# Block 2's expert loop: ScalarE and VectorE each split two neighbouring weight chunks in one operation of 2048 columns instead of one chunk in an operation of 1024

## The reference, cut to what matters

```python
def run_block(args):
    tok, e = args
    xb = hf[jnp.minimum(tok, n_tok - 1)]
    a = xb @ w_gate[e]
    b = xb @ w_up[e]
    return (jax.nn.silu(a) * b) @ w_down[e]
```

## Time and profile before

| | us |
|---|---|
| time before, median of 3 runs | 2129.56 |
| lowest and highest run | 2127.35 and 2130.23 |
| span of the profiled execution, first to last instruction | 2122.2 |
| TensorE matmul busy in it | 2024.8 (95%) |
| VectorE busy | 1678.8 (79%) |
| ScalarE busy | 1229.4 (58%) |
| GpSimd busy | 468.0 (22%) |

### The profile page before, as it was taken

How to read it: one execution, slowest core, us unless ns; L and a number is a source line. 1 busy time by engine, 2 the same in 40 slices (tenths; PEclk the granted TensorE clock), 3 DMA queues, 4 the chain that set the end, 5 groups by cost and what they waited for, 6 DMA issues and landing times.

```text
span 2122.2 us, 31552 instructions
## 1 busy us (share of the span) xinstructions
PE 2024.8 (95%) x9690; PEld 1676.1 (79%) x9690; DVE 1678.8 (79%) x1905; ACT 1229.4 (58%) x1453; POOL 468.0 (22%) x368
## 2 busy tenths in 40 slices
PE   5999999969999999999999999999999999999996
PEld 4888888858888878787778787888888888887873
DVE  6676755488999999999856455548999999999994
ACT  5211113216888787878644533224888888888872
POOL 1000001101010101010010253111344444444442
PEclk9999999959999999999999999999999999999998
DMA  9476844439999999999821112355999999999996
GB/s 353 143 233 220 266 179 167 174 135 338 380 379 388 377 389 377 390 377 390 319 75 54 37 41 105 114 186 203 384 383 383 370 381 378 372 378 363 379 361 242
DMA packets 234184, 592.52 MB, mean 279 GB/s; under 512 B 23936, under 2 KB 61076, under 8 KB 234109
## 3 DMA queue, kind: packets, MB, share of 16 engines
q1 hardware_dynamic: 210400, 527.50, 66.4%
q0 software_dynamic: 22640, 61.32, 9.8%
q10 hardware_dynamic: 1068, 2.73, 0.3%
HBM read 560.57 MB, written 50.91 MB: 288 GB/s over the span
## 4 chain that ended last, share of the span: by engine, by line
PE 64%; DMA 15%; DVE 8%; SPq 6%; issue 3%; ACT 2%; POOL 0%; POOLq 0%; ACTq 0%; DVEq 0%
PE ps L2377 19%; PE ps L2380 18%; PE ps L2378 18%; DMA ring<-in_moe_w_up 6%; SPq L575 6%; DMA ring<-in_w_expert_up 4%; DMA ring<-in_moe_w_down 1%; DVE mL L2301 1%; PE ps L2862 1%; PE ps L2532 1%; DVE mL L1777 1%; PE ps L2693 1%; DMA ring<-in_ada_w 1%; PE ps L2385 1%; DVE mL L2217 1%
## 5 line engine op out<-in xcount | busy, mean ns | idle before, releaser
L2217 DVE TENSOR_TENSOR mL<-ring,mH 128x1024 fp32r<-128x1024 f32 x384 | 479.3, 1288 | 21.6 <-ACT mH L1381 20.0
L1777 DVE TENSOR_TENSOR mL<-ring,mH 128x1024 fp32r<-128x1024 f32 x384 | 455.3, 1220 | 32.3 <-ACT mH L1189 22.8
L1189 ACT ACTIVATE mH<-ring 128x1024 fp32r<-128x1024 f32 x384 | 401.9, 1062 | 100.0 <-PE ps L2380 65.0
L1381 ACT ACTIVATE mH<-ring 128x1024 fp32r<-128x1024 f32 x384 | 394.9, 1056 | 65.4 <-PE ps L2380 21.5
L2377 PE MATMUL ps<-mH,xsH 128*128 128x512 f32 x1056 | 423.0, 401 | 2.2 <-DVE mL L2217 1.4
L2380 PE MATMUL ps<-mH,xsL 128*128 128x512 f32 x1056 | 413.3, 391 | 0.0
L2378 PE MATMUL ps<-mL,xsH 128*128 128x512 f32 x1056 | 411.0, 389 | 0.0
L2380 PEld LDWEIGHTS ps<-mH,xsL 128*128 128x128 f32 x1056 | 198.2, 188 | 43.5
L2377 PEld LDWEIGHTS ps<-mH,xsH 128*128 128x128 f32 x1056 | 198.7, 188 | 41.3 <-DVE mL L2217 1.6
L2378 PEld LDWEIGHTS ps<-mL,xsH 128*128 128x128 f32 x1056 | 198.9, 188 | 38.1
L2377 PE MATMUL ps<-mH,hidH 128*128 128x512 f32 x528 | 209.7, 397 | 7.8 <-DVE hidL L1832 6.4
(11 more groups left out here) (474 smaller groups left out, 3209.0 us busy)
## 6 DMA issues: line engine op xcount, KB each, us to landing
ring<-in_w_expert_gate SPq DMA_DIRECT2D x140, 512.0 KB, 11.2
ring<-in_w_expert_up SPq DMA_DIRECT2D x140, 512.0 KB, 11.4
ring<-in_w_expert_down SPq DMA_DIRECT2D x140, 512.0 KB, 12.5
ring<-in_moe_w_gate SPq DMA_DIRECT2D x128, 512.0 KB, 12.2
ring<-in_moe_w_up SPq DMA_DIRECT2D x128, 512.0 KB, 12.1
ring<-in_moe_w_down SPq DMA_DIRECT2D x128, 512.0 KB, 13.3
ring<-in_ada_w SPq DMA_DIRECT2D x96, 512.0 KB, 7.2
ring<-in_sc_w_in SPq DMA_DIRECT2D x24, 512.0 KB, 9.0
```

Source lines behind the costliest of these rows:

```text
L1189: act.activation(mH[:, m % WSETS, :], ring[:, m % RING, :], ACT.Copy).then_inc(S["m1_hi"], 1)
L1381: act.activation(mH[:, wset, :], ring[:, slot, :], ACT.Copy).then_inc(S["m2_hi"], 1)
L1777: dve.tensor_tensor(mL[:, m % WSETS, :], ring[:, m % RING, :], mH[:, m % WSETS, :].bitcast(F32), ALU.subtract).then_inc(S["m1_lo"], 1)
L2217: dve.tensor_tensor(mL[:, wset, :], ring[:, slot, :], mH[:, wset, :].bitcast(F32), ALU.subtract).then_inc(S["m2_lo"], 1)
```

## The change

`m2_hi` and `m2_lo` now take two neighbouring chunks, n and n + 1 with n even, in one operation of 2048 columns. The high part waits for both landings and for the buffers of both (n + 1 - 6 multiplied); `m2_hi` and `m2_lo` count by two when the whole operation is done. Both are called for even c alone. `EARLY2` goes from 3 to 2; in the opening ScalarE makes 0 and 1, then 2 and 3, then after the token's high parts 4 and 5, and VectorE makes 0 and 1 before the last routing operations and leaves 2 and 3 to the loop's step 0. What stands before an odd c stays where it was in the order, so silu and the hidden product now follow the pair (0, 1), and the first token part follows the pair (8, 9). The overflow blocks, TensorE, GpSimd and SyncE are left as they are.

```diff
--- before.py
+++ after.py
@@ -19,7 +19,7 @@
 RING = 12
 SPLIT_RING = 6
 EARLY1 = 4
-EARLY2 = 3
+EARLY2 = 2
 ADA_RING = 6
 WSETS = 6
 E1 = 16
@@ -1375,12 +1375,13 @@
 
         def m2_hi(q, r, c):
             n, slot, wset, turn = m2_at(q, r, c)
-            act.wait_ge(ring_in[slot], 16 * (used2[slot] + turn + 1))
+            for u in range(2):
+                act.wait_ge(ring_in[slot + u], 16 * (used2[slot + u] + turn + 1))
             if not (static(q) and n < WSETS):
-                act.wait_ge(S["m2_used"], n - WSETS + 1 + past["m2_used"])
-            act.activation(mH[:, wset, :], ring[:, slot, :], ACT.Copy).then_inc(S["m2_hi"], 1)
-
-        for c in range(EARLY2):
+                act.wait_ge(S["m2_used"], n + 1 - WSETS + 1 + past["m2_used"])
+            act.activation(mH[:, wset:wset + 2, :], ring[:, slot:slot + 2, :], ACT.Copy).then_inc(S["m2_hi"], 2)
+
+        for c in range(0, EARLY2, 2):
             m2_hi(0, 0, c)
 
         def x_hi2(e, r, j):
@@ -1398,11 +1399,10 @@
                            scale=slot_w[:, bass.ds(e, 1)]).then_inc(S["m2_y"], 1)
 
         act.wait_ge(S["tok_tr"], 2 + past["tok_tr"])
-        for c in (3, 4):
-            m2_hi(0, 0, c)
+        m2_hi(0, 0, 2)
         for j in range(2):
             x_hi2(0, 0, j)
-        m2_hi(0, 0, 5)
+        m2_hi(0, 0, 4)
         act.wait_ge(S["rows_known"], 1)
 
         def m2_step(q, r):
@@ -1424,7 +1424,7 @@
                                    ACT.Copy).then_inc(S["m2_hT_hi"], 1)
                 if c in (9, 11) and not (static(q) and s >= E2):
                     x_hi2(s + 1, 1 - r, (c - 9) // 2)
-                if not (static(q) and (s == 0 and c < WSETS or s == E2 and c < 8)):
+                if c % 2 == 0 and not (static(q) and (s == 0 and c < WSETS or s == E2 and c < 8)):
                     m2_hi(q, r, c)
             if static(q) and s == 0:
                 for j in range(2):
@@ -2213,9 +2213,9 @@
 
         def m2_lo(q, r, c):
             n, slot, wset, _ = m2_at(q, r, c)
-            dve.wait_ge(S["m2_hi"], n + 1 + past["m2_hi"])
-            dve.tensor_tensor(mL[:, wset, :], ring[:, slot, :], mH[:, wset, :].bitcast(F32),
-                              ALU.subtract).then_inc(S["m2_lo"], 1)
+            dve.wait_ge(S["m2_hi"], n + 2 + past["m2_hi"])
+            dve.tensor_tensor(mL[:, wset:wset + 2, :], ring[:, slot:slot + 2, :], mH[:, wset:wset + 2, :].bitcast(F32),
+                              ALU.subtract).then_inc(S["m2_lo"], 2)
 
         def x_lo2(e, r, j):
             dve.wait_ge(S["m2_xT_hi"], 2 * e + j + 1 + past["m2_xT_hi"])
@@ -2245,8 +2245,6 @@
                                       op0=ALU.mult, op1=ALU.add))
         dve.tensor_copy(row_of[:, 0:NBLK], slot_t[:, 1, :]).then_inc(S["rows_known"], 1)
         dve.wait_ge(S["rows_known"], 2)
-        for c in range(1, EARLY2):
-            m2_lo(0, 0, c)
         for j in range(2):
             x_lo2(0, 0, j)
 
@@ -2274,7 +2272,7 @@
                     x_lo2(s + 1, 1 - r, (c - 9) // 2)
                 if c == 11 and static(q) and s == E2 - 1:
                     hidden(s, r)
-                if not (static(q) and (s == 0 and c < EARLY2 or s == E2 and c < 8)):
+                if c % 2 == 0 and not (static(q) and (s == 0 and c < EARLY2 or s == E2 and c < 8)):
                     m2_lo(q, r, c)
             if static(q) and s == 0:
                 for j in range(2):
```

## The result

The changed kernel takes 2136.32 us (median of 5 runs, 2133.44 to 2137.61) beside 2129.24 us for the kernel before in runs shared with it: a ratio of 1.0038, with a 95% interval of 1.0027 to 1.0050. It is slower, by 0.38% or some 8 us (7.1 between the two medians). The time lies in the forecast's range, but the loss isn't the 1 us of the forecast, and it is more than the 0.2% that I had called no change. The profiled execution has a span of 2131.8 us, 9.6 more than before. A run's time is 1.6 us longer than its span (2133.44 us for this one), so the profiled execution of the kernel before would be a run of 2123.8 us, 5.4 under the median, and that of the kernel after is 2.9 under its own. The profiles thus show a difference 2.5 us larger than that of the medians, and a term of 1 or 2 us read between two of them is not settled by that alone.

What follows compares the result with a forecast made beforehand. PE was taken as the bound early, with the late steps following the loads. Late steps, end and opening summed as 0 + 1.9 - 0.9 + 0 = +1.0 us, set on the median 2129.56: 2130.6 us, range 2126 to 2143.

Steps and rivals of the forecast that it cites:

- Operations: Wide operations in the loop: 1.92 us for a high part on ScalarE, 2.28 us for a low part on VectorE.
- early steps: Early loop steps: PE never waits for a pair and keeps about 17.8 us a step, cost 0.
- Rival B: Early steps lose their cover at pair (0, 1) and the hidden rows' low part: about 2140 to 2160 us, chance 0.15.
- If landings stay where they are: Late steps: the longer chain from chunk 7 to the hidden rows' low part costs 1.9 us once, bounds 0 to 1.9 plus 1.2.
- What the pairing moves: List of one early step's pairs: each is ready 1.0 to 2.3 us before PE needs it, cost 0.
- I read the landing time as a queue: Weight loads: DMA engines are always busy, so a load issued 1 to 3 us later lands at the same time.
- Rival C: Late loads take 14 to 16.7 us whenever issued; seven late steps grow by 1.9 us, +13, about 2143 us, chance 0.10.
- "Cost 0" for GpSimd: Gate product's thirds and scatter come later in the step; each third adds up to 0.73 us to a pair, covered.
- The opening: Before and in step 1: first matmul about 1 us earlier, some 2 us wait before c = 0; net 0, -0.4 to +1.
- The end: After the last hidden rows only pair (10, 11) remains, so the overflow begins earlier: -0.9 us, between -1.4 and 0.
- A: The forecast itself: PE's early steps untouched, about 1 us lost late; 2127 to 2134 us, chance 0.62.
- D: Fewer loads in flight are served better and 2.7 us of late stalls go: -3.9 us, about 2125.5, chance 0.13.

Runs made afterwards that it cites:

- down_single: The kernel after with VectorE's low parts of c = 8 to 11 single again: 2133.62 us, ratio 1.0036.
- late_issue: The kernel before, with SyncE issuing an even chunk's load only together with its odd neighbour's: 2127.54 us, ratio 1.0005.
- eight_after: The kernel after with eight split buffers instead of six: 2134.55 us, ratio 1.0037.
- gates_early: The kernel after with the three waits that pace GpSimd's gate product each one event earlier: 2138.10 us, ratio 1.0052.
- eight_before: The kernel before with eight split buffers instead of six: 2127.59 us, ratio 1.0000.
- scatter_late: The kernel before, with GpSimd's scatter held back until the low part of the next step's c = 1: 2165.58 us, ratio 1.0183.
- light_after: The kernel after with the loads of c = 9 and 11 cut to half their columns: 2125.75 us, ratio 0.9993.

## Why the prediction was right or wrong, step by step

- **Operations** (1.92 and 2.28 us) and **early steps** (0, at 17.78 us a step): right. 231.31 and 231.33 us from step 1 to 14. Rival B doesn't occur here; down_single shows it, at 0.2 us a step, where VectorE is 98% busy. That the loads go out 1 to 3 us later was right too, 2.5 on average. VectorE's low parts take 28.9 us less (479.3 to 450.4), where the forecast had some 12.
- **"If landings stay where they are, PE ends the loop later by the difference, 1.9 us, once and not in each step"**: this failed: the late steps lost 6.5 us, over the 3.1 that its own bounds allow. The chain that it priced, c = 7 and the hidden rows' low part, has the operations at their forecast sizes and lost only 0.6 us more than before. The step that failed is the place of the wait: 5.9 us are lost at the pairs (8, 9), (10, 11) and (0, 1), where the list "What the pairing moves" had 1.0 to 2.1 us to spare. That list took no landing into account, and a pair of which one landing is late holds up both of its chunks.
- **"I read the landing time as a queue in front of engines that are always busy, so that a load issued somewhat later lands at the same time"**: half right. Issue time is indeed worth little: about 1 us in late_issue, and nothing to be gained in eight_after. Rival C is not there either; the trace of the kernel after gives no landing times, but ScalarE waits for no landing between 1500 and 1700 us. What the reading had wrong is what makes a landing late. A mean busy share of 1.00 over sixteen engines doesn't say that each part of a load waits in the same queue: before, the last part comes some 9 us behind the eighth late in the loop. With wide low parts a packet takes 151 ns instead of 148, 2% more, already in steps 2 to 14, in which PE has not stalled at all, so that a stall isn't its cause. That this is what makes the last parts later isn't shown. From 1500 to 2000 us the kernel before moves 1882 x 100 (384 + 377 + 378 + 377 + 366, in GB/s us) and the kernel after 1859 x 100, 2.3 MB or 6 us of loading less, but a loop that is 6 to 8 us behind also loads that much less; in steps 2 to 14, ahead of any stall, the load queue moves 349.6 GB/s instead of 350.3.
- **"Cost 0" for GpSimd**: its thirds are covered as written, and moving them alone gains nothing (gates_early). But its two row transfers take 4.4 instead of 2.8 us a step, which the prediction hadn't looked at. I don't count it as shown that they slow the loads: in the table packet time and transfer time rise together over most kernels, but eight_before has 3.4 us at 148.3 ns and down_single 3.3 us at 150.4. In scatter_late, with single low parts alone, 8.3 us go with 155.5 ns.
- **The opening, "0, between -0.4 and +1"**: failed at 1.3 us net, of which -0.84 is the first matmul's place, which varies by more than that. The wait was right (2.22 for "some 2 us"). The step's missing term was the clock behind the wait, 1.58 us.
- **The end, -0.9**: VectorE's part was right (0.7 nearer), but it was not the last chain. The output copy and the gather behind it were, 1.2 us later; the stretch from step 31 to the end is 1.75 us longer in all, 0.9 of it still waits for loads.
- That the range held the result is luck. A alone had 2127 to 2134, under the 2136.32 measured; the upper part stood there for rivals C and B, and neither happened. D's faster late loads did not happen either. The chance of a slower kernel was put at 0.29. The Trainium skill, Perfetto Trace Analysis, section "Optimizing Scalar/DVE Operations", had spoken for the slower side: where an engine isn't saturated but causes bubbles, break instructions up. The runs agree on the side for VectorE (1.0008 with single low parts under wide high parts against 1.0038), and not for ScalarE, whose single high parts gave nothing back (1.0040).

What stays open is why the wide low parts slow the load packets. Two causes are left: GpSimd's row transfers, which take 4.4 us a step instead of 2.8, and the long operations themselves. Telling them apart needs both kernels with the row transfers replaced by plain ones; that wasn't tried. Nor is it settled how the 6.5 us divide between later last parts and the pair's longer chain, since both act only where landings are late. No kernel of the study that does the whole computation beats the kernel before.

## What to carry to other kernels

An operation that is merged is freed and delivered by its last part: ask at each place where its input arrives late, not only where the engine was busy. Where PE already follows the loads, price the pair at every place where one of its two landings can be late, not at the one that was last before. A mean busy share of 1.00 doesn't say when a load lands: a load counts as landed with its last part, so look at the last count beside the share and GB/s. A wait that grows on PE should be checked for the clock behind it, and an engine's order should be checked at the end of the loop as well as in its middle.

## What the runs showed that I had not expected

- TensorE's granted clock fell from 1.00 to 0.50 behind a wait of 2.22 us, in the middle of dense matmuls, and stayed there some 3 us, in the kernel after and four others; with the same wait in light_after it did not fall.
- A row scatter on GpSimd took 1.60 us, 2.3 to 2.7 us beside wide low parts and 7.37 us beside a gapless run of single ones on VectorE.
- The mean load packet took 148 to 149 ns with single low parts and 151 to 153 ns with wide ones, at a mean DMA busy share of 1.01 to 1.02 in both (steps 2 to 14). With single low parts and the scatter of 7.37 us it took 155.5 ns.
- In the kernel before, the last sixteenth of a load came 0.9 us behind the eighth early in the loop and some 9 us behind it late.
